# Expert-table blocks loaded as one 1 MB transfer into two neighbouring ring slots, in place of two of 512 KB

## The reference, cut to what matters

```python
e = i1[ci // 16] * 128 + i2[ci % 16]        # 128 chosen experts per token, of 16384
g = softmax(cv)
a = einsum('ckd,cd->ck', u_emb[ec], hc)     # hc: one token's normed row
coef = gelu(a) * gc
out = einsum('ck,ckd->cd', coef, v_emb[ec])
```

## Time and profile before

| | us |
|---|---|
| median of 3 runs | 3778.07 (3764.3 to 3783.99) |
| profiled execution, its own time | 3762.47 |
| its span | 3760.7 |
| TensorE busy | 3304.1 (88%) |
| VectorE busy | 2900.7 (77%) |
| ScalarE busy | 1430.8 (38%) |
| GpSimd busy | 1158.8 (31%) |
| DMA, mean over the span | 302 GB/s |

### The profile page before, as it was taken

One profiled execution on the slowest core, in us unless ns is written; L12 is line 12 of the kernel. 1 busy time (PEld: TensorE's weight loads), 2 busy tenths in 40 slices (PEclk: granted clock), 3 DMA queues, 4 the chain that ended last, 5 costly groups with the idle time before them and its releaser, 6 DMA issues.

```text
span 3760.7 us, 46481 instructions
## 1 busy us (share of the span) xinstructions
PE 3304.1 (88%) x18296; PEld 2825.9 (75%) x18296; DVE 2900.7 (77%) x3547; ACT 1430.8 (38%) x2000; POOL 1158.8 (31%) x773
## 2 busy tenths in 40 slices
PE   8998999998899989999997555899999999899950
PEld 7876667777788867789997555677789999777740
DVE  5664787877789878878884233899888888899887
ACT  5555676554422223433322111344323333344320
POOL 0000000011123323312778877232222222232246
PEclk9999999999999999999998887999999999999975
DMA  8863988676699999974666566999999999999999
GB/s 283 279 215 121 305 308 282 199 277 229 244 382 396 387 366 354 379 285 134 136 148 148 127 164 178 358 389 393 376 395 408 409 411 374 378 402 385 375 362 351
DMA packets 345288, 1137.02 MB, mean 302 GB/s; under 512 B 63088, under 2 KB 79856, under 8 KB 273648
## 3 DMA queue, kind: packets, MB, share of 16 engines
q1 hardware_dynamic: 226336, 547.43, 41.9%
q0 software_dynamic: 110592, 537.05, 38.7%
q10 hardware_dynamic: 8144, 49.58, 3.3%
HBM read 1106.54 MB, written 27.39 MB: 302 GB/s over the span
## 4 chain that ended last, share of the span: by engine, by line
PE 50%; POOL 14%; DVE 14%; DMA 13%; issue 5%; ACT 4%; SPq 0%; ACTq 0%; DVEq 0%; POOLq 0%
PE ps L1394 28%; POOL c_dense L482 11%; PE ps L1656 9%; DMA w<-v_emb 7%; PE ps L1675 7%; DVE w_lo L895 4%; PE ps L1634 3%; POOL rows L493 3%; ACT w_hi L512 2%; DMA rows<-v_emb,eidx 2%; DVE acc L920 2%; DMA c_dense<-gsel,cidx 1%; DVE rows L912 1%; PE ps L1487 1%; DMA w<-w_out 1%
## 5 line engine op out<-in xcount | busy, mean ns | idle before, releaser
L512 ACT ACTIVATE w_hi<-w 128x1024 fp32r<-128x1024 f32 x752 | 797.1, 1061 | 1245.2 <-PE ps L1394 731.9
L895 DVE TENSOR_TENSOR w_lo<-w,w_hi 128x1024 fp32r<-128x1024 f32 x752 | 916.9, 1223 | 361.0 <-ACT w_hi L512 354.5
L1394 PE MATMUL ps<-w_hi,ht_all 128*128 128x512 f32 x3328 | 836.4, 395 | 21.2 <-ACT w_hi L512 16.7
L493 POOL DMA_INDIRECT rows<-u_emb,eidx x256 | 306.9, 1199 | 1671.7 <-DVE dots L912 910.8
L920 DVE SCALAR_TENSOR_TENSOR acc<-rows,coef,acc 128x2048 f32<-128x2048 f32 x256 | 601.2, 2348 | 225.3 <-DMA rows<-v_emb,eidx 222.5
L1394 PEld LDWEIGHTS ps<-w_hi,ht_all 128*128 128x128 f32 x3328 | 626.1, 190 | 160.7 <-issue 12.9
L493 POOL DMA_INDIRECT rows<-v_emb,eidx x256 | 406.9, 1589 | 710.2 <-DVE acc L920 665.0
L912 DVE CUSTOM_DVE_ANT_0 rows<-rows,h 128x2048 f32<-128x2048 f32 x256 | 584.1, 2282 | 5.1 <-DMA rows<-u_emb,eidx 4.7
L1656 PE MATMUL ps<-ht_all,w_hi 128*128 128x256 f32 x4096 | 561.1, 290 | 1.5 <-ACT w_hi L854 1.5
L1656 PEld LDWEIGHTS ps<-ht_all,w_hi 128*128 128x128 f32 x4096 | 515.4, 194 | 2.1 <-issue 1.7
L482 POOL DMA_INDIRECT c_dense<-gsel,cidx x256 | 443.0, 1730 | 206.0 <-DVEq L1327 100.6
(11 more groups left out here) (200 smaller groups left out, 2479.0 us busy)
## 6 DMA issues: line engine op xcount, KB each, us to landing
w<-w_in SPq DMA_DIRECT2D x320, 512.0 KB, 4.7
w<-u_emb SPq DMA_DIRECT2D x256, 512.0 KB, 6.5
w<-v_emb SPq DMA_DIRECT2D x256, 512.0 KB, 8.5
w<-w_out SPq DMA_DIRECT2D x64, 512.0 KB, 5.7
w<-w_pq SPq DMA_DIRECT2D x64, 512.0 KB, 7.4
c_dense<-zeros ACTq DMA_DIRECT2D x16, 1024.0 KB, 6.4
w<-w_br_b SPq DMA_DIRECT2D x32, 512.0 KB, 6.1
c_ring<-c_dense SPq DMA_DIRECT2D x64, 256.0 KB, 8.8
```

What stands on the lines that cost most here:

```text
L493: pool.indirect_dma_start(rows[:, n % ROWS, :], None, (u_emb, v_emb)[table], bass.IndirectOffsetOnAxis(ap=eidx[:, tile, k:k + 1], axis=0)) ...
L512: act.activation(w_hi[:, g % 2, :, :], w[:, SLOT[g], :, :], ACT.Copy).then_inc(hi_ready, 1)
L895: dve.tensor_tensor(w_lo[:, g % 2, :, :], w[:, SLOT[g], :, :], w_hi[:, g % 2, :, :].bitcast(F32), ALU.subtract).then_inc(lo_ready, 1)
L1394: ins = pe.matmul(ps[:, seg.bank + t, :], lhs(t)[:, half, k, :], wt[:, g % 2, kk, :], start=(j == 0 and part == 0 and kk == 0), stop=(j == ...
```

## The change

It adds a function and changes three places. A block's load is issued once, at its even slab, as 1 MB into two neighbouring slots; its wait is for the prior slab of the odd slot. Its landing is counted on the even slot's semaphore, and the readers of either slab (ScalarE's hi in the v stages, TensorE's turn in the u stages) wait on that one. The projections' loads stay as they are: they are slabs before `U_G0[0]`.

```diff
+def load_of(g):
+
+    return g if g < U_G0[0] else g - g % 2
+
...
-                        sp.wait_ge(lo_ready, SLOT_PRIOR[g0 + j] + 1)
-                        sp.dma_start(w[:, SLOT[g0 + j], :, :].rearrange("p k c -> p (k c)"),
-                                     blocks[HB * h + j // 2, :, D // 2 * (j % 2):D // 2 * (j % 2 + 1)]).then_inc(w_loaded[SLOT[g0 + j]], 16)
+                        if j % 2 == 0:
+                            s = SLOT[g0 + j]
+                            sp.wait_ge(lo_ready, SLOT_PRIOR[g0 + j + 1] + 1)
+                            sp.dma_start(w[:, s:s + 2, :, :].rearrange("p s k c -> p (s k c)"), blocks[HB * h + j // 2, :, :]).then_inc(w_loaded[s], 16)
...
             def hi(g):
-                act.wait_ge(w_loaded[SLOT[g]], 16 * SLOT_USE[g])
+                first = load_of(g)
+                act.wait_ge(w_loaded[SLOT[first]], 16 * SLOT_USE[first])
                 need(act, slab_done, g - 1)
                 act.activation(w_hi[:, g % 2, :, :], w[:, SLOT[g], :, :], ACT.Copy).then_inc(hi_ready, 1)
...
             def turn_block(h, i):
                 g = U_G0[h] + i
-                pe.wait_ge(w_loaded[SLOT[g]], 16 * SLOT_USE[g])
+                first = load_of(g)
+                pe.wait_ge(w_loaded[SLOT[first]], 16 * SLOT_USE[first])
                 pe.wait_ge(lo_ready, g - 1)
```

## The result

| | before | after |
|---|---|---|
| median, 4 runs each | 3781.0 us (3764.3 to 3794.6) | 3863.0 us (3834.1 to 3872.7) |
| ratio | 1 | 1.0206 (95%: 1.0138 to 1.0275) |
| profiled execution | 3762.5 us | 3872.7 us |

The change makes the kernel about 2% slower; 3872 had been forecast. The profiled execution is the slowest of the four after, so the 110 us between the two profiles stand for a median difference of 82. The size is less sure than the interval says: in the three later sets the kernel before had medians of 3763 to 3766 us, and against those 3863.0 is 2.6% slower. In kernel.py after the change L468 is the load, L519 and L902 hi and lo in the v stages, L861 and L907 in the u stages, L1642 TensorE's turn.

The account below looks back on a forecast made before the run. It took the v stages as bound by the four-slot ring's used-up lead, u half 1 by TensorE. Terms 78 + 10 + 4 + 2 = +94 us, on the 3778.1 us median, gave 3872 us, 2.5% slower; range 3760 to 3975.

Parts of the forecast that it names:

- The ring's loop bounds the v stages: v stages before the change: four slabs per turn of load, hi and lo, 11.8 us; the ring's lead is used up.
- signs named beforehand: v stages: hi waits about once per pair, at even slabs, 1 us or more; windows 35 to 45 us longer each.
- The lead taken away: Ring of w slots: the even slab's load waits for lo(e-3) instead of lo(e-4), one slab later.
- L': Time from issue to landing of a 1 MB load: 7.5 us in the v stages, bounds 5.5 and 8.1.
- the v stages at +78: Both v halves: 66 pairs with a row turn in the even slab lose 1.18 us each, 62 pairs nothing.
- The share of the queues: Loads beside gathers: queues alternate packet by packet; 8 KB packets raise q1 from a third to half, 200 GB/s.
- rival 3: Loads: 8 KB rows go as two 4 KB packets, share unmoved; v +141, u half 1 +82, 4000 us; chance 0.10.
- the sign named beforehand: Queues q1 and q0: equal packets and equal bytes in a shared microsecond.
- u half 1 at +10: u half 1: landing 8.1 against lead 7.85, late by 0.25 us; +8, with scatter +10; bounds 0 and +82.
- u half 0, scatter, start of v half 1, tail: u half 0: loads cost nothing, GpSimd's scatter waits +4 us; start of v half 1 +2; tail 0.
- Rival 1: Loads: a megabyte lands within 6 us, so the kernel gets faster, returning at most 34 us: 3744; chance 0.12.
- The sum: Whole kernel: 78 + 10 + 4 + 2 = +94 us.

Follow-up runs that it names:

- e1: Against the kernel before: still two 512 KB loads per block, but both issued only when the odd slab's slot is free; 3845.3 us, ratio 1.0211.
- e5: Against the changed kernel: 1 MB pair loads kept, six ring slots in expert half 1; 3763.8 us, ratio 1.0010 to the kernel before.
- e6: Against the kernel before: 512 KB loads kept, six ring slots in expert half 1; 3753.0 us, ratio 0.9969.
- e2: Against the changed kernel: a block's slabs go into slots two apart, so 1 MB arrives in 4 KB pieces; 3982.6 us, ratio 1.0593 to the kernel before.
- e4: Against the kernel before: 1 MB loads in the two u stages only; 3801.8 us, ratio 1.0121.
- e8: Against the changed kernel: most gathers fetch 1 KB per token in place of 8 KB; 3734.0 us, ratio 0.9926 to the kernel before.
- e3: Against the kernel before: 1 MB loads in the two v stages only; 3822.8 us, ratio 1.0151.

## Why the prediction was right, point by point

**The ring's loop bounds the v stages.** Right, and shown from both sides: a slab less of lead lengthens them (e1), two slots more shorten v half 1 (e5, e6). Of the signs named beforehand, hi waits for the load 46 and 44 times in 64 pairs, at even slabs, as forecast; the v windows are 25 and 33 us longer, not 35 to 45. The prediction also took the DMA engines' 99% for a sign that the stage was near the loaded end. That was wrong: with more slots the same loads and gathers ran at 403 to 408 GB/s instead of 380, so 0.99 was no bound on throughput.

**The lead taken away.** Right: e1, which does this alone, costs 2.1%, and with two slots more the loss of the change is gone (e5).

**L', and the v stages at +78.** The forecast was 7.5 us; measured 6.7 and 7.1, and +58 us. The loop itself holds: over both stages two pairs take 12.6 and 12.9 us, and landing plus slot time, measured load by load, are 6.6 + 6.0 and 7.1 + 5.8. But how the loss was to fall on the pairs is wrong. The step said that 66 pairs lose 1.18 us each and 62 nothing. Timed from the lo of one even slab to that of the next, the pairs with a turn in the even slab went from 6.10 to 6.42 us (65 of them, 21 us in all), and the others from 5.78 to 6.37 (61, 36 us in all): those that were to lose nothing lost more. Their loads landed later, after 7.1 and 7.7 us on average, than those of the pairs with a turn, after 6.3 and 6.4, and the time from landing to the end of the second lo was 5.1 and not 4.3 on average (6.6 where there is a turn, as forecast). One mean L' for both kinds hid this: put into the formula, 6.9 gives 66 x 0.88 = +58 for one kind, but with TensorE's 5.6 as a floor also -19 for the other, +39 together. Why the two kinds differ in their landings was not tested. The loop spans two pairs, so a delay in one can be paid in the next; that is argued, not shown.

L' itself was high because 4.6 us had been put down for the transfer, and its packets took 4.0 to 4.2.

**The share of the queues.** Right in part. Over a load in u half 1 q1's share rose from 36 to 54%, and the rows are 8 KB packets, so rival 3 is out. e2 puts a price on the packet size, 3 to 4% of the kernel. But the sign named beforehand, equal packets and equal bytes in a shared microsecond, is not what the trace shows: the queues move largely in bursts, and in u half 1 the share is the same 55% with 4 KB packets. So "turns packet by packet, hence half" is not shown as the cause there. By the Trainium skill ("DMA: Bandwidth & Descriptors", Queues, rings and completion order) an engine goes round its queues by whole packets. The 35 against 35 before agrees with it, if a record is a packet; the bursts after (96 records against 5, then 16 against 90) do not, unless a packet is several records. The records do not tell the engine, so this stays open.

**u half 1 at +10.** This step failed in size: +57 in this profile, +46 in e4, inside its bounds of 0 and 82. I took L' as 8.1, "rows present throughout", with a quarter of a microsecond of lateness; it was 9.0 on average against the lead of 7.85, and (9.0 - 7.85)/2 x 64 = 37. Load by load, half of every lateness beyond 7.85 adds up to 43 us (the early loads give nothing back), against 41 us of gaps; the other 17 us are longer work, the larger part the clock (below), which the step did not price. What 8.1 left out is the time before the first packet: 2.9 us had been put down for all that is fixed, and it was 3.0 before the first packet and 1.0 after the last; the transfer took 5.0, and 5.2 was forecast. e8 bears this out: with thin gathers the first packet came after 1.6 us and the landing after 6.1.

**u half 0, scatter, start of v half 1, tail.** Forecast +4, +2 and 0; measured +1 with its gap, -3 and -6. The loads of u half 0 landed after 5.3 us, below the 5.5 that was the lower bound for a megabyte. GpSimd waited 26.5 us for its scatters, against 27.9: the larger packets beside them did nothing that can be seen. The -6 of the tail is not explained; e4 has 128.7 there and e3 135.2, so it may be how far the gathers lag when the tail begins. That is argued, not shown.

**Rival 1 and the rule on 1 MiB.** Refuted here. The Trainium skill (same page, section Bandwidth) says to batch to 1 MiB or more for at least 75% of the peak; the price of 2.0 us and bytes/436 GB/s stands in its section on the anatomy of one DMA, as a fit for transfers issued from GpSimd. A part that does not grow with the size is real in this trace: nearly alone, 512 KB lands in 4.2 us and 1 MB in 5.0 (medians of u half 0). But loads that overlap in a ring do not pay it one after the other; what counts is when the slot was free and when the first slab of the block can be read.

**The sum** came out as 94 against 110 in the profiles and 82 in the medians, with one term too large by 20 and one too small by 47. The forecast of the time was good partly by luck: these two largely cancel, and in the v stages a wrong split over the pairs still gave a fair sum.

## What to carry to other kernels

In a ring of n slots a transfer over two slots takes one slab of lead from the first of them and makes it wait for the second's data: with four slots that is a third of the lead of three slabs. Write the loop down first, (slots/slabs per load) x time per load = landing + the time in which a slot is held, and see whether landing fits with the engines' own pace; if it doesn't, more slots are worth more than fewer transfers. If the loads share the DMA engines with another queue, try longer contiguous pieces: 8 KB in place of 4 KB was worth 45 and 26 us in the v stages here, and did not change the landing in u half 1. And when two queues are to be shown sharing, look at several short windows in a row; one laid across a change-over shows equal bytes that were never shared.

## What the runs showed of the hardware

A short stall can cost TensorE more than its length. At 2958.4 us of the changed kernel it stood idle for 2.7 us, and the next slab's 24 products took 4.37 us in place of 2.88. Windows at 2961 and 2963:

```profile
2961.00:2963.00 2.00, 1.89 (x15) 1.89 (x16) 0.00 (x0) 0.76 (x1) 0.30 (x1) 0.88 0.91 352
2963.00:2965.00 2.00, 2.00 (x11) 2.00 (x11) 1.71 (x2) 0.26 (x1) 0.00 (x0) 0.50 1.01 401
```

0.50 is 1.2 GHz of 2.4. Not every stall does it: at 2979.7 us, after 1.9 us idle, the next products took 2.88. What decides it was not tested. Over u half 1 the granted clock went from 0.99 to 0.97, and in e2, with longer stalls, to 0.93.
